# Dense layer's last chunk to attention's projection: token tiles, column modulation, head pairs, unrolled chunks

## The reference

```python
def swiglu(t, w_gu, w_down):
    g, u = jnp.split(t @ w_gu, 2, axis=-1)
    return (jax.nn.silu(g) * u) @ w_down

# end of layer 0
y = swiglu(h, ffn_w_gu[j], ffn_w_down[j])
x = x + gate2[:, None] * rms_norm(y, norm_g[0, 3])
# layer 1: attention
h = rms_norm(x, norm_g[1, 0]) * (1.0 + scale1[:, None]) + shift1[:, None]
q, k, v = jnp.split(h @ w_qkv, 3, axis=-1)      # 8 heads, two components of 64 in q and k, 128 in v
s = q k^T * 64**-0.5 + bias(distance), causal;  p = softmax(s)
a = p[:, :, 0] - lam * p[:, :, 1]
o = rms_norm(a @ v, subln_g) * (1.0 - lambda_init)      # over the 128 channels of a head
y = o.reshape(B, S, D) @ w_o
x = x + gate1[:, None] * rms_norm(y, norm_g[1, 1])
```

## Time and profile before

| | us |
|---|---|
| median of 3 runs (1413.78 to 1415.28) | 1413.79 |
| the profiled execution, its own time | 1416.15 |
| its span | 1414.2 |
| PE busy | 1342.8 (95%) |
| DVE busy | 1175.4 (83%) |
| ACT busy | 893.9 (63%) |
| POOL busy | 77.6 (5%) |

### The profile page before, as it was taken

The page is one execution under the profiler, slowest core; times in us unless marked ns, Lnnn a source line. Parts: engine busy times, 40 slices in busy tenths (PEclk is TensorE's granted clock), DMA queues, the critical chain, the costliest instruction groups (busy, mean ns, idle before and its releaser), DMA issues.

```text
span 1414.2 us, 19749 instructions
## 1 busy us (share of the span) xinstructions
PE 1342.8 (95%) x6877; PEld 1128.8 (80%) x6877; DVE 1175.4 (83%) x947; ACT 893.9 (63%) x730; POOL 77.6 (5%) x91
## 2 busy tenths in 40 slices
PE   5589999999889999999999999999999999999995
PEld 4489999779667888888888888888888888888883
DVE  5877677798768988889888889888888888898883
ACT  3144343344737777777777777777777777777771
POOL 2510000010020000000000000000000000000000
PEclk9689999999999999999999999999999999999998
DMA  9998788859067999999999999999999999999970
GB/s 363 382 349 300 251 296 294 283 197 409 24 237 249 408 397 378 371 389 382 355 397 386 357 396 369 387 363 395 387 344 401 380 364 387 373 390 360 411 289 32
DMA packets 210262, 476.63 MB, mean 337 GB/s; under 512 B 14920, under 2 KB 38544, under 8 KB 210208
## 3 DMA queue, kind: packets, MB, share of 16 engines
q1 hardware_dynamic: 205216, 459.07, 87.0%
q0 software_dynamic: 4992, 16.86, 3.9%
HBM read 466.95 MB, written 8.93 MB: 337 GB/s over the span
## 4 chain that ended last, share of the span: by engine, by line
PE 85%; DVE 10%; issue 2%; ACT 1%; DMA 1%; POOL 0%; SPq 0%; DVEq 0%; POOLq 0%; ACTq 0%
PE ps L1515 27%; PE ps L1517 27%; PE ps L1516 27%; PE ps L1864 2%; DVE wlo L1011 1%; DVE rows L1108 1%; DVE rows L1103 1%; DVE rows L1023 1%; DVE rows L1025 1%; DMA raw<-w_mod 1%; ACT whi L691 1%; DVE wlo L1293 1%; PE ps L1533 1%; PE ps L1830 0%; PE ps L1821 0%
## 5 line engine op out<-in xcount | busy, mean ns | idle before, releaser
L1293 DVE TENSOR_TENSOR wlx<-raw,whx 128x2048 fp32r<-128x2048 f32 x168 | 384.8, 2292 | 97.6 <-ACT whx L903 96.7
L1293 DVE TENSOR_TENSOR wlo<-raw,whi 128x2048 fp32r<-128x2048 f32 x168 | 384.2, 2288 | 4.8 <-ACT whi L903 3.3
L903 ACT ACTIVATE whi<-raw 128x2048 fp32r<-128x2048 f32 x168 | 322.3, 1920 | 88.6 <-PE ps L1517 87.5
L903 ACT ACTIVATE whx<-raw 128x2048 fp32r<-128x2048 f32 x168 | 322.3, 1920 | 82.8 <-PE ps L1517 82.8
L1515 PE MATMUL ps<-whi,thi 128*128 128x512 f32 x508 | 203.7, 401 | 1.2 <-DVE wlo L1282 1.1
L1517 PE MATMUL ps<-whi,tlo 128*128 128x512 f32 x508 | 198.5, 391 | 0.0
L1516 PE MATMUL ps<-wlo,thi 128*128 128x512 f32 x508 | 198.2, 390 | 0.0
L1515 PE MATMUL ps<-whx,thi 128*128 128x512 f32 x452 | 176.8, 391 | 0.0
L1517 PE MATMUL ps<-whx,tlo 128*128 128x512 f32 x452 | 176.2, 390 | 0.0
L1516 PE MATMUL ps<-wlx,thi 128*128 128x512 f32 x444 | 172.9, 389 | 0.0
L1515 PE MATMUL ps<-thi,whi 128*128 128x256 f32 x480 | 137.3, 286 | 3.3 <-DVE tlo L1015 3.3
(11 more groups left out here) (248 smaller groups left out, 1913.5 us busy)
## 6 DMA issues: line engine op xcount, KB each, us to landing
raw<-moe_w_gu SPq DMA_DIRECT2D x448, 512.0 KB, 5.9
raw<-moe_w_down SPq DMA_DIRECT2D x224, 512.0 KB, 6.4
raw<-w_mod SPq DMA_DIRECT2D x96, 512.0 KB, 6.5
raw<-ffn_w_gu SPq DMA_DIRECT2D x44, 512.0 KB, 4.7
raw<-w_qkv SPq DMA_DIRECT2D x24, 512.0 KB, 6.2
raw<-ffn_w_down SPq DMA_DIRECT2D x22, 512.0 KB, 5.0
raw<-w_o SPq DMA_DIRECT2D x8, 512.0 KB, 7.0
gain<-norm_g POOLq DMA_DIRECT2D x5, 512.0 KB, 5.3
```

The lines of the kernel that those rows point to most:

```text
L903: act.activation(m_hi[m % MRING], raw[:, r % RAW, :], ACT.Copy).then_inc(hi_ready, 1)
L1293: dve.tensor_tensor(m_lo[m % MRING], raw[:, r % RAW, :], m_hi[m % MRING].bitcast(F32), ALU.subtract).then_inc(unit_done, 1)
```

## The change

What it does, part by part:

1. **The loop over chunks is unrolled** on all four engines, and the `w_mod` units are dealt out anew (`FFN_MODS`, `QKV_MODS`): none in step 0, two in most steps, three in the last two; 20 in the dense layer where there were 18, and 8 in QKV where there were 10, none of these behind the first group.
2. **The last down product goes tile by tile of tokens**: t = 0 whole, then t = 1, and each tile's square, gate and residual (`residual_tile`) follow on their own.
3. **Scale and shift become columns.** Instead of row sums, PE makes `column_sums` (8 small matmuls each, one per channel block), and DVE finishes them in two small instructions. DVE only multiplies x by the inverse root; the transposed blocks are scaled and shifted per channel on ACT (`modulate_tile`, 16 activations of 128x128), which then takes `thi` by tile and half; DVE takes `tlo` from SBUF.
4. **The first QKV group is v0** (`QKV_ORDER`), run tile by tile, each tile by halves of the channels. The bias pieces 0 to 2 are multiplied around the transposes, into banks 0 to 2, and piece 3 into bank 3, behind the first group. ACT copies all four out behind `modulate_tile`, ahead of the split of the second group's units.
5. **Heads are normalized by pairs**: pair 0 and 1 within the loop over heads, 2 and 3 behind it. Two row sums move ahead of the last two heads' values. The transposes of the first four heads precede the last values; those of the last four stand between the second and third unit of the projection at t = 0, and `w_o`'s units are ordered by channel half first.

The core of the diff:

```diff
-LOOP_MODS = [[(1, 0, 0), (1, 1, 0)], [(1, 2, 0)], [(1, 0, 1), (1, 1, 1)], [(1, 2, 1)]]
-TAIL_MODS = [[(0, 5, 0), (0, 5, 1), (0, 5, 2)], [(0, 5, 3), (1, 3, 0), (1, 3, 1)]]
-QKV_MODS = [[(1, 3, 2), (1, 3, 3)], [(1, 4, 0), (1, 4, 1)], [(1, 4, 2), (1, 4, 3)], [(1, 5, 0), (1, 5, 1)],
-            [(1, 5, 2), (1, 5, 3)], []]
+FFN_MODS = [[], [(1, 0, 0), (1, 0, 1)], [(1, 0, 2), (1, 0, 3)], [(1, 1, 0), (1, 1, 1)], [(1, 1, 2), (1, 1, 3)],
...
+QKV_MODS = [[], [(1, 4, 0), (1, 4, 1)], [(1, 4, 2), (1, 4, 3)], [(1, 5, 0), (1, 5, 1)], [(1, 5, 2), (1, 5, 3)], []]
+QKV_ORDER = (4, 0, 1, 2, 3, 5)
...
# ACT
-            act.wait_ge(unit_used, Q_QKV)
-            square_y(1)
-            finish_shift(1, 0)
+            def modulate_tile(t, b):
+                act.wait_ge(ht_ps, 4 + 2 * t + b + 1)
+                for k in range(4 * b, 4 * b + 4):
+                    act.activation(hv3[:, k, t * P:t * P + P], ps[:, 4 + 2 * t + b, (k % 4) * P:(k % 4) * P + P], ACT.Identity,
+                                   scale=modc[:, 0, k:k + 1], bias=modc[:, 1, k:k + 1]).then_inc(ht_v, 1)
+                act.wait_ge(ht_v, KC + 8 * t + 4 * b + 4)
+                act.activation(thi3[:, 4 * b:4 * b + 4, t * P:t * P + P], hv3[:, 4 * b:4 * b + 4, t * P:t * P + P],
+                               ACT.Copy).then_inc(ht_hi, 1)
...
             square_x(2)
+            act.wait_ge(col_ready, 6)
+            for t in range(T):
+                for b in range(2):
+                    modulate_tile(t, b)
             act.wait_ge(ss_ready, 4 * 2 + T)
             for b in range(4):
                 act.wait_ge(bias_ps, b + 1)
-                act.copy(bias_t[:, 2 * b:2 * b + 2, :], bank(4 + b).rearrange("p (h k) -> p h k", h=2)).then_inc(bias_ready, 1)
-            high_transposed(2)
+                act.copy(bias_t[:, 2 * b:2 * b + 2, :], bank(b).rearrange("p (h k) -> p h k", h=2)).then_inc(bias_ready, 1)
...
             high(R_WO, Q_WO)
             at_copy(NH - 1)
             o_copy(NH - 2)
+            turned_heads(0)
+            turned_heads(1)
             o_copy(NH - 1)
             high(R_WO + 1, Q_WO + 1)
             finish_shift(1, 3)
-            for b in range(4):
...
+            turned_heads(2)
+            turned_heads(3)
             high(R_WO + 2, Q_WO + 2)
# DVE
+            for t in range(T):
+                residual_tile(0, 5, t, T, 6 + t)
+            dve.wait_ge(col_ps, 6)
+            dve.scalar_tensor_tensor(modc[:, 0, :], ps[:, 3, 0:KC], 1.0, cols[:, 8, :], ALU.add, ALU.mult).then_inc(col_ready, 1)
+            dve.tensor_copy(modc[:, 1, :], ps[:, 3, KC:2 * KC]).then_inc(col_ready, 1)
+            for t in range(T):
+                rs = inverse_root(2, t)
+                dve.wait_ge(x_done, T + t + 1)
+                dve.tensor_scalar(hs[:, t, :], xs[:, t, :], rs, None, ALU.mult).then_inc(h_ready, 1)
...
-                if h == NH - 2:
+                if h == 4:
                     head_eps(0)
-            head_square(NH - 3)
-            head_norm(0)
-            low(R_WO, Q_WO)
...
+                if h == 5:
+                    head_norm(0)
+                if h == 6:
+                    head_eps(1)
# PE
-            ffn_down(NCF - 1, R_LAST_DOWN, Q_LAST_DOWN, last=True)
-            row_sum(1, 1)
+            for t in range(T):
+                for jj in range(2):
...
+                mm.then_inc(unit_used if t else down_ps, 1)
             pe.wait_ge(row_done, done_rank(0, 5))
-            row_sum(1, 0)
+            column_sums(1, 1, ps[:, 3, 0:KC])
+            column_sums(1, 0, ps[:, 3, KC:2 * KC])
...
+            bias(0)
+            turn_normalized(0)
+            bias(1)
+            bias(2)
+            turn_normalized(1)
...
+            for t in range(T):
+                for kh in range(2):
+                    pe.wait_ge(ht_lo, 4 + 2 * t + kh + 1)
+                    if t == 0:
+                        pe.wait_ge(unit_done, R_GROUP[0] + kh + 1)
...
+                    if t:
+                        mm.then_inc(unit_used, 1)
+            pe.wait_ge(col_ready, 6)
+            bias(3)
+            for g in range(1, 5):
                 qkv_group(g)
...
+                if h == NH - 1:
+                    pe.wait_ge(sc_max, NH)
+                    row_sum(1, 2)
+                    row_sum(1, 3)
                 if h > 0:
                     values(h - 1)
+            pe.wait_ge(row_done, done_rank(1, 2))
+            turn_heads(0)
+            turn_heads(1)
             values(NH - 1)
-            row_sum(1, 2)
-            row_sum(1, 3)
             pe.wait_ge(o_ready, T * NH)
             row_sum(1, 4)
...
+                for u in range(4):
+                    half, kh = u % 2, u // 2
+                    if t == 0:
+                        if u == 2:
+                            pe.wait_ge(shift_done, done_rank(1, 3))
+                            turn_heads(2)
+                            turn_heads(3)
+                        pe.wait_ge(unit_done, R_WO + u + 1)
```

More of the change, by code:

```diff
@@ L855, in _, with turned_heads @@
                     o_copy(h - 2)
+            def turned_heads(b):
+                act.wait_ge(ot_ps, b + 1)
+                act.activation(thi[:, 512 * b:512 * b + 512], bank(b), ACT.Copy, scale=subln[:, 1:2]).then_inc(ot_hi, 1)
             high(R_WO, Q_WO)
```

379 lines of the change are left out of this document (172 added, 207 removed).

## The result

| | us, median | ratio to before, 95% interval |
|---|---|---|
| before (4 runs) | 1414.53 | |
| changed (4 runs) | 1427.97 | 1.0098 [1.0081, 1.0116] |

The profiled execution of the changed kernel took 1430.54 (span 1428.7, mean granted clock 0.973), that of before 1416.15 (1414.2, 0.979): +14.4. The experts take as long as before; all of the difference is there when the projection's first tile is summed.

The account below looks back on a forecast made before the run. PE bounds the experts; ahead of QKV a serial ACT, POOL and DVE chain does. Terms -0.5 - 4.7 + 5.9 + 5.6 + 2.0 = +8.3 on 1413.79 gave 1422 us, range 1414.5 to 1426.

Parts of the forecast that it names:

- both waits: PE waiting behind the first QKV group, +5.9 us, and between the projection's units at the end of attention, +5.6 us.
- Unrolling and dealing: Dense layer: the loop branch's 0.46 us stall goes, the 1.04 us stall in a three-unit step stays; -0.5 us.
- The reason given, the branch: Dense layer: the 0.46 us stall behind the loop's first turn was said to belong to the loop's branch.
- First QKV product: Last down product to QKV: tile-by-tile work lets the first product start at 289.7 instead of 294.39, -4.7 us.
- Behind the first group: QKV: ACT's fourth bias copy waits for PE's last bias piece and delays the second group's splits; +5.9 us.
- The loop over heads: Attention: DVE gets 1.0 us more work, mostly hidden; the projection's first unit starts 2.75 us before 395.55.
- Between the projection's units: End of attention: second and third units wait for late weight splits, so the first tile's sum comes 5.6 us later.
- The 4.2 for the normalizations: End of attention: the last eight normalizations on DVE meet POOL's loads and memset again and take 4.2 us.
- the 6.1 in front of the third unit: Projection: activations, ACT's split and DVE's split take 6.1 us, in which PE has only eight transposes.
- The granted clock: Behind three idle stretches: half-clock spells of 3.4 us, costing up to 5.1 us together; taken as +2.0 us.
- The rival that let the clock take all: Three half-clock spells lie wholly on dense work: +11.4 us, 1425.2; counted in the forecast's 0.64, no separate chance.

## Why the prediction was too low

Slower was right, and both waits stood where it put them; 1422 was 6 us too low, and 1427.97 is 2 above the range. Step by step:

- **Unrolling and dealing, -0.5.** From the first gate-and-up product the dense layer took 0.46 us less (84.80 to 274.96; 84.33 to 274.95 before), but it began 0.47 later, so nothing is left. That start lay anywhere from 82.98 to 85.05 in the traces, so I don't charge it to the change. The reason given, the branch, was wrong: unrolled alone, the kernel keeps the stall. That the layer took about 0.5 less all the same was luck.
- **First QKV product, -4.7.** It was -3.7. The transposes began at 285.81, as forecast. But the clock was at half from 285.4 to 288.8, a spell like that of the earlier trace rows. There it lay on bias pieces that nobody waited for; here the transposes and pieces are what the first product waits for. The first eight transposes took 1.97, where I had taken full speed from 16 in 1.97 (the second eight, at full clock, took 1.04), and two bias pieces and the second tile's transposes then held PE from 287.6 to 290.7, though the first `tlo` was ready. So this 1.0 is the clock's too. The spell began within an idle stretch of only 0.64, behind 16 column sums of one column each and a bias piece:

```profile
285.00:290.00 5.00, 4.36 (x14) 2.88 (x14) 2.29 (x4) 3.67 (x10) 0.79 (x2) 0.66 0.00 0
```

- **Behind the first group, +5.9.** 5.67 from the group's end to the next product, with the chain as told: piece, copy, ACT's split, DVE's. Right, and undone by moving one piece. The group itself, 512 wide, took 0.4 less than the one that was first before.
- **The loop over heads, -2.75 for the first unit.** -2.2, with 0.7 lost to the clock in the row sums (against the two traces in which the spell there was 3.4 us long and not 6.8). Right.
- **Between the projection's units, +5.6 from the attention's start (+8.4 from the first unit).** +12.1 was measured, 3.1 of it clock, so 9.0. The 4.2 for the normalizations (4.10) and the 6.1 in front of the third unit (6.1 from the second unit's last transposes at 409.06) were right.
- **The granted clock, +2.0. This step failed.** It gave each wait a spell of 3.4 us at most, of which part should lie in the idle time, with 5.1 as the bound. Two of the three lay wholly on dense work. The first did begin in the idle time, but was 6.8 long and had 5.2 on dense work. Together they cost 5.4 us, and two spells for which the sum had nothing cost 1.0 ahead of the first product and 0.7 in the row sums: 7.1 in place of 2.0, which is 5.1 of the 6.0 us missed. The rest is 0.5 by which the dense layer began later, 0.6 of the regrouped products, which the sum had at nothing, and 0.6 in the projection, less 0.8 in the other steps.

The rival that let the clock take all, 1425.2, came nearest, and it too counted 3.4 us per wait. The error was to read one spell, in a gap where it cost nothing, as the size of every spell, and to look for spells behind long waits only. The kernel before has a longer one in its own trace, at the start of the dense layer, where PE was idle for 3.15 us (5 us at a mean of 0.80, then 5 at 0.52, some 6.8 us at half), and I hadn't read it:

```profile
80.00:85.00 5.00, 1.85 (x14) 1.79 (x14) 3.26 (x4) 3.51 (x7) 3.46 (x5) 0.80 0.97 371
85.00:90.00 5.00, 5.00 (x26) 5.00 (x26) 2.13 (x4) 4.55 (x7) 1.35 (x2) 0.52 0.85 303
```

The Trainium skill (TensorE: Matmul & The Clock Gate, "What's actually happening") has the gate follow how busy PE has been recently. The trace agrees: each of the three waits, of 3.6 us or more, went with a clock of 0.50 to 0.52. The prediction had the rule, and took 2.0 all the same.

## What to carry to other kernels

In an instruction list that runs in order, a small instruction moved behind a long group moves everything that is queued behind its reader: here one matmul of 1.0 us held a copy, two splits and PE for 5.7. An idle stretch of PE of 3.6 to 5.0 us ahead of dense work cost, beside the wait, 1.5 to 2.3 us for the clock; look too at small work on the path, such as transposes, that a spell can fall on. Short fixes to the order won back what the change lost and 3.4 us more; products of zeros in the idle stretches took 6.6 us off, and between column sums or behind an idle stretch they cost time.

## What the runs showed of the hardware

- An idle stretch of PE of 2.5 to 5.0 us went with a clock at half for 3.4 us, 6.8 or 10.2, from within the stretch or from just behind it. Its length alone didn't decide. In the changed kernel it was 6.8 us with 4.8 idle, and 3.4 with 3.6 and 5.0. The 5.04 ahead of the projection's third unit had 3.4 there and 6.8 with POOL's work moved. The 3.15 at the start of the dense layer had 6.8 in the kernel before and 10.2 in the changed one. The 2.47 in the loop over heads had 6.8 in the changed kernel and 3.4 where the first wait was filled.
- No spell came directly behind 1.3 idle or less in the projection, but one of 3.4, from 285.4, began in an idle stretch of 0.64, behind 16 column sums of one column (3.63 us) and a bias piece.
- POOL's root of 128x4 took 2.98 us where DVE split a weight unit at the same time, and 1.01 in its next use:

```profile
393.53 2.98 POOL L605 TENSOR_TENSOR oss<-oss,minus_half 128x4 f32<-128x4 f32 x1 [6.28 <-DVE oss L1219]
...
397.11 1.01 POOL L605 TENSOR_TENSOR oss<-oss,minus_half 128x4 f32<-128x4 f32 x1 [0.60 <-DVE oss L1219]
```

  DVE's split ran from 393.36 to 395.64. The root had started inside it and ended 0.87 behind it. Whether the split held it isn't tested: no run moves the one away from the other.
